# Where the activations lie in SBUF: 64 bytes later, and 272-token tiles 1,152 bytes apart

## The reference

```python
def first_block(...):                       # 272 tokens
    h = concatenate([meta, x])
    h += _mixer_rglru_swa(rmsnorm(h) ...)   # in0: projection, recurrence, windowed attention; out0
    h += swiglu(rmsnorm(h) ...)             # gu0: 1024 -> 2 x 2816, dn0: 2816 -> 1024
    h += _mixer_retention(rmsnorm(h) ...)   # in1: 1024 -> 6144, out1: 2048 -> 1024
    h += swiglu(rmsnorm(h) ...)             # gu1, dn1 (256 tokens from here on)
    return h[:, N_META:]

def second_block(x, ...):                   # 256 tokens, two layers
    x += 0.5 * rms_norm(swiglu(rms_norm(x), ffn1...))
    x += rms_norm(hybrid_mixer(rms_norm(x) ...))      # three attentions, gates, w_out
    x += 0.5 * rms_norm(swiglu(rms_norm(x), ffn2...))

def swiglu(x, wg, wu, wd):
    return (silu(x @ wg) * (x @ wu)) @ wd
```

## Time and profile before

| what | value |
|---|---|
| median of three runs | 2012.21 us |
| profiled execution, first to last instruction (span) | 2011.9 us |
| PE busy | 1998.7 us, 99% |
| PEld busy | 1755.0 us, 87% |
| DVE / ACT / POOL busy | 59% / 49% / 15% |
| mean granted TensorE clock | 0.997 |
| HBM read | 341.10 MB, 170 GB/s over the span |

### The profile page before, as it was taken

How to read it: one execution, slowest core, us unless ns; L and a number is a source line. 1 busy time by engine, 2 the same in 40 slices (tenths; PEclk the granted TensorE clock), 3 DMA queues, 4 the chain that set the end, 5 groups by cost and what they waited for, 6 DMA issues and landing times.

```text
span 2011.9 us, 27800 instructions
## 1 busy us (share of the span) xinstructions
PE 1998.7 (99%) x11810; PEld 1755.0 (87%) x11810; DVE 1178.9 (59%) x1133; ACT 990.8 (49%) x1076; POOL 303.7 (15%) x204
## 2 busy tenths in 40 slices
PE   9999999999999999999999999999999999999998
PEld 8899999999999988887888888888888888888887
DVE  6854446757654455546566865546555556686553
ACT  6753334345544354445356564446444535666443
POOL 4034401514344010002100110001000210011000
PEclk9999999999999999999999999999999999999999
DMA  7345556544555555554543445554556554354553
GB/s 223 105 138 176 167 179 201 168 129 144 186 177 181 188 187 184 185 197 159 176 147 126 167 168 188 188 209 159 185 180 209 168 167 146 112 209 154 183 180 136
DMA packets 195587, 343.67 MB, mean 171 GB/s; under 512 B 14122, under 2 KB 97356, under 8 KB 195356
## 3 DMA queue, kind: packets, MB, share of 16 engines
q1 hardware_dynamic: 194844, 340.12, 51.3%
q0 software_dynamic: 368, 0.79, 0.2%
q10 hardware_dynamic: 272, 1.26, 0.2%
HBM read 341.10 MB, written 1.05 MB: 170 GB/s over the span
## 4 chain that ended last, share of the span: by engine, by line
PE 91%; DVE 4%; ACT 3%; DMA 1%; POOL 1%; issue 0%; SPq 0%; DVEq 0%; POOLq 0%; ACTq 0%
PE banks L557 18%; PE banks L560 17%; PE banks L558 17%; PE banks L397 7%; PE banks L399 7%; PE banks L398 7%; PE banks L448 5%; PE banks L1778 2%; PE banks L1779 2%; PE banks L1780 2%; DVE w_lo L391 1%; PE banks L596 1%; PE banks L1869 1%; PE banks L1871 1%; PE banks L1870 1%; ACT w_hi L375 1%
## 5 line engine op out<-in xcount | busy, mean ns | idle before, releaser
L391 DVE TENSOR_TENSOR w_lo<-raw,w_hi 128x2048 fp32r<-128x2048 f32 x307 | 730.5, 2382 | 514.5 <-ACT w_hi L375 514.0
L375 ACT ACTIVATE w_hi<-raw 128x2048 fp32r<-128x2048 f32 x311 | 593.8, 1913 | 648.3 <-DMA raw<-ffn_wd 149.6
L557 PE MATMUL banks<-w_hi,xn_hi 128*128 128x512 f32 x1192 | 471.9, 396 | 0.9 <-DVE xn_lo L818 0.5
L558 PE MATMUL banks<-w_lo,xn_hi 128*128 128x512 f32 x1192 | 464.1, 389 | 0.0
L560 PE MATMUL banks<-w_hi,xn_lo 128*128 128x512 f32 x1192 | 459.6, 390 | 0.0
L557 PEld LDWEIGHTS banks<-w_hi,xn_hi 128*128 128x128 f32 x1192 | 223.9, 188 | 49.3 <-DVE w_lo L391 3.0
L560 PEld LDWEIGHTS banks<-w_hi,xn_lo 128*128 128x128 f32 x1192 | 223.8, 188 | 47.6
L558 PEld LDWEIGHTS banks<-w_lo,xn_hi 128*128 128x128 f32 x1192 | 224.1, 188 | 44.0
L397 PE MATMUL banks<-xn_hi,w_hi 128*128 128x272 f32 (+1 forms) x720 | 208.4, 289 | 0.5 <-DVE w_lo L1162 0.5
L399 PE MATMUL banks<-xn_hi,w_lo 128*128 128x272 f32 (+1 forms) x720 | 207.1, 288 | 0.0
L398 PE MATMUL banks<-xn_lo,w_hi 128*128 128x272 f32 (+1 forms) x720 | 206.7, 287 | 0.0
(11 more groups left out here) (371 smaller groups left out, 3079.1 us busy)
## 6 DMA issues: line engine op xcount, KB each, us to landing
raw<-w_in SPq DMA_DIRECT2D x58, 1024.0 KB, 5.1
raw<-ffn_wd SPq DMA_DIRECT2D x44, 1024.0 KB, 4.8
raw<-ffn_w_gu SPq DMA_DIRECT2D x42, 1024.0 KB, 4.9
raw<-ffn_wu SPq DMA_DIRECT2D x40, 1024.0 KB, 5.0
raw<-ffn_wg SPq DMA_DIRECT2D x35, 1024.0 KB, 5.0
raw<-ret_w_in SPq DMA_DIRECT2D x24, 1024.0 KB, 5.1
raw<-ffn_w_down SPq DMA_DIRECT2D x22, 1024.0 KB, 4.8
raw<-ret_w_out SPq DMA_DIRECT2D x8, 1024.0 KB, 5.4
```

Source lines behind the costliest of these rows:

```text
L375: nc.scalar.activation(hi_of(n0), raw_of(n0), ACT.Copy).then_inc(hi_done(n0), 1)
L391: nc.vector.tensor_tensor(lo_of(n0), raw_of(n0), hi_of(n0).bitcast(F32), ALU.subtract).then_inc(lo_done(n0), 1)
L557: pe.matmul(ps[:, (b + n) * 512:(b + n + 1) * 512], xh, h, start=start, stop=False)
L558: pe.matmul(ps[:, (b + n) * 512:(b + n + 1) * 512], xh, o, start=False, stop=False)
```

## The change

Three things are done to the byte offsets, and the order and number of instructions stay as they were on each engine.

1. 64 bytes are skipped ahead of `hT`, so `hT`, `xn_hi`, `xn_lo`, `act_hi` and `act_lo` start at 64 modulo 512 (`act_lo` is now placed by `act_hi` being rounded to the phase of `hT`), `Y` and the constants behind it at 320. The weights stay at 0, and the extra chunks (`raw_x`, `lo_x`, `hi_x`) that lie inside the activations' memory are rounded up to a multiple of 512 of their own. The split attention output (`mo_hi`, `mo_lo`) is at 64 in all three places. The first two chunks of gu0, staged raw in `act_hi`'s memory, land at 64.
2. Tiles of 272 tokens in `xn_*` and `act_*` are 288 words (1,152 bytes) apart: tile k starts at 64 + 128 k modulo 512, an odd multiple of 64 for every k. In part of the retention projection, which starts 16 tokens (64 bytes) into the tile, the start becomes 128 (k + 1), an even multiple for every k. `y1_split` keeps its packed tiles.
3. Copies over several tiles now step over the gap: ScalarE's copy of 128x544 becomes 128x2x272, GpSimd's and VectorE's subtraction likewise, and one copy and one subtraction of 128x1088 become 128x4x272.

```diff
+TS = 288
...
+A_PHASE = 64
...
-            if name in ("act_hi", "act_lo"):
-                at[0] += (raw_at - at[0]) % 512
+            if name == "act_hi":
+                at[0] += (hT_at - at[0]) % 512
...
-        hT, _ = new("hT", [P, KT, T1])
-        xn_hi, xn_at = new("xn_hi", [P, KT * T1], F32R)
-        xn_lo, _ = new("xn_lo", [P, KT * T1], F32R)
-        act_hi, a_at = new("act_hi", [P, NFF * T1], F32R)
-        act_lo, _ = new("act_lo", [P, NFF * T1], F32R)
+        at[0] += A_PHASE
+        hT, hT_at = new("hT", [P, KT, T1])
+        xn_hi, xn_at = new("xn_hi", [P, KT * TS], F32R)
+        xn_lo, _ = new("xn_lo", [P, KT * TS], F32R)
+        act_hi, a_at = new("act_hi", [P, NFF * TS], F32R)
+        act_lo, _ = new("act_lo", [P, NFF * TS], F32R)
...
-        raw_x, lo_x, hi_x = ([... for b, at0 in enumerate((extra_at, a_at))]
+        raw_x, lo_x, hi_x = ([... for b, at0 in enumerate((extra_at - extra_at % 512 + 512, a_at - a_at % 512 + 512))]
...
-        mo_hi, mo_lo = ([... (qn_at, vn2_at, e2_at)[x] ...
+        mo_hi, mo_lo = ([... (qn_at, vn2_at, e2_at + (a_at - e2_at) % 512)[x] ...
...
-                last = product(e, ..., xn_hi[:, kt * t:(kt + 1) * t], xn_lo[:, kt * t:(kt + 1) * t], ...)
+                last = product(e, ..., trow(xn_hi, kt, t), trow(xn_lo, kt, t), ...)
...
-                    c = (xt0 + 2 * k + j) * t
+                    c = (xt0 + 2 * k + j) * pitch(t)
...
+        def pitch(t):
+            return TS if t == T1 else t
+        def trow(x, kt, t, lo=0):
+            return x[:, kt * pitch(t) + lo:kt * pitch(t) + t]
+        def trows(x, kt, n, t):
+            return x[:, kt * pitch(t):(kt + n) * pitch(t)].rearrange("p (k s) -> p k s", s=pitch(t))[:, :, 0:t]
...
-                    at0 = (k0 - 1) * t
-                    dst = act_hi[:, at0:at0 + 2 * t] ...
-                    act.activation(dst, g, ACT.Copy).then_inc(S["ah"], 1)
+                    st = pitch(t)
+                    at0 = (k0 - 1) * st
+                    dst = act_hi[:, at0:at0 + 2 * st] ...
+                    act.activation(tiles(dst, st)[:, :, 0:t], tiles(g, t), ACT.Copy).then_inc(S["ah"], 1)
...
-                pool.tensor_tensor(lo, g, hi.bitcast(F32), ALU.subtract).then_inc(S["al"], 1)
+                pool.tensor_tensor(tiles(lo, st)[:, :, 0:t], g3, tiles(hi, st)[:, :, 0:t].bitcast(F32),
+                                   ALU.subtract).then_inc(S["al"], 1)
...
-                    xh, xl = xn_hi[:, kt * T1 + lo:(kt + 1) * T1], xn_lo[:, kt * T1 + lo:(kt + 1) * T1]
+                    xh, xl = trow(xn_hi, kt, T1, lo), trow(xn_lo, kt, T1, lo)
```

More of the change, by code:

```diff
@@ L229, in build_program @@
         extra_at = y_at + 4 * 7 * D
[L230 removed]
+        raw_x, lo_x, hi_x = ([place(f"{name}{b}", [P, CH], dt, at0 + off) for b, at0 in enumerate((extra_at - extra_at % 512 + 512, a_at - a_at % 512 + 512))]
                              for name, dt, off in (("raw_x", F32, 0), ("lo_x", F32R, 0), ("hi_x", F32R, 4 * CH)))
@@ L275, in build_program @@
         e2, p2, t1b, t2b = layer_map(e2_at, [("e2", [P, 4 * 384]), ("p2", [P, 4 * 384]), ("t1b", [P, 4, T2]), ("t2b", [P, 4, T2])], y_end)
-        mo_hi, mo_lo = ([place(f"mo_{part}{x}", [P, 4 * T2], F32R, (qn_at, vn2_at, e2_at)[x] + q * 16 * T2) for x in range(3)]
+        mo_hi, mo_lo = ([place(f"mo_{part}{x}", [P, 4 * T2], F32R, (qn_at, vn2_at, e2_at + (a_at - e2_at) % 512)[x] + q * 16 * T2) for x in range(3)]
                         for q, part in enumerate(("hi", "lo")))
@@ L496, in act_fill @@
                     act.wait_ge(S["pe_chunk"], base)
-                act.activation(xn_hi[:, kt * t:(kt + 1) * t], hv(kt, off, t), ACT.Copy,
+                act.activation(trow(xn_hi, kt, t), hv(kt, off, t), ACT.Copy,
                                scale=gcol[:, g0 + kt:g0 + kt + 1]).then_inc(S["xh"], 1)
@@ L504, in dve_fill @@
             dve.wait_ge(S["xh"], 8 * f + kt + 1)
-            c = slice(kt * t, (kt + 1) * t)
-            dve.scalar_tensor_tensor(out=xn_lo[:, c], in0=hv(kt, off, t), scalar=gcol[:, g0 + kt:g0 + kt + 1],
-                                     in1=xn_hi[:, c].bitcast(F32), op0=ALU.mult, op1=ALU.subtract).then_inc(S["xl"], 1)
+            dve.scalar_tensor_tensor(out=trow(xn_lo, kt, t), in0=hv(kt, off, t), scalar=gcol[:, g0 + kt:g0 + kt + 1],
+                                     in1=trow(xn_hi, kt, t).bitcast(F32), op0=ALU.mult, op1=ALU.subtract).then_inc(S["xl"], 1)
         def dve_residual(w, fill=None, off=0, t=T1, between={}):
@@ L1078, in fill_hi @@
                 act.wait_ge(S["xT"], kt + 1)
-                act.activation(xn_hi[:, kt * T1:(kt + 1) * T1], ps[:, kt * 512:kt * 512 + T1], ACT.Copy,
+                act.activation(trow(xn_hi, kt, T1), ps[:, kt * 512:kt * 512 + T1], ACT.Copy,
                                scale=gcol[:, G_MIX0 + kt:G_MIX0 + kt + 1]).then_inc(S["xh"], 1)
@@ L1165, in first_fill @@
                 dve.wait_ge(S["xh"], kt + 1)
-                c = slice(kt * T1, (kt + 1) * T1)
-                dve.scalar_tensor_tensor(out=xn_lo[:, c], in0=ps[:, kt * 512:kt * 512 + T1], scalar=gcol[:, G_MIX0 + kt:G_MIX0 + kt + 1],
-                                         in1=xn_hi[:, c].bitcast(F32), op0=ALU.mult, op1=ALU.subtract).then_inc(S["xl"], 1)
+                dve.scalar_tensor_tensor(out=trow(xn_lo, kt, T1), in0=ps[:, kt * 512:kt * 512 + T1],
+                                         scalar=gcol[:, G_MIX0 + kt:G_MIX0 + kt + 1], in1=trow(xn_hi, kt, T1).bitcast(F32), op0=ALU.mult, op1=ALU.subtract).then_inc(S["xl"], 1)
             dve.wait_ge(S["vecT"], 1)
@@ L1658, in heads_hi @@
                 act.wait_ge(S["pv0"], g + 1)
-                at0, b = (4 + 2 * g) * T1, GROUP_BANKS[g][0]
-                act.activation(tiles(xn_hi[:, at0:at0 + 2 * T1], T1), bank(b, 2)[:, :, 0:T1], ACT.Copy).then_inc(S["xcat_h"], 1)
+                b = GROUP_BANKS[g][0]
+                act.activation(trows(xn_hi, 4 + 2 * g, 2, T1), bank(b, 2)[:, :, 0:T1], ACT.Copy).then_inc(S["xcat_h"], 1)
             split_hi(base + 2, 0)
@@ L1708, in act_l0 @@
             act.wait_ge(S["scan"], 1)
-            act.activation(tiles(xn_hi[:, 0:4 * T1], T1), lt[:, :, :], ACT.Copy).then_inc(S["yrnh"], 1)
+            act.activation(trows(xn_hi, 0, 4, T1), lt[:, :, :], ACT.Copy).then_inc(S["yrnh"], 1)
             split_hi(out0 + 2, 0)
```

32 lines of the change are left out of this document (16 added, 16 removed).

## The result

The changed kernel is slower. It takes 2034.28 us, the median of 4 runs (2033.01 to 2036.71), against 2011.99 us for the kernel before (4 runs, 2011.77 to 2013.87). The ratio is 1.011, with a 95% interval of 1.0097 to 1.0122, so 22.3 us more where the forecast was 17.3 less. The two profiled executions lie closer together, since that of before was its slowest and that of after its fastest: 2013.87 against 2033.01 us, spans of 2011.9 and 2031.2. (A span is 1.8 to 2.0 us shorter than the time of the same execution.

A forecast was written before the change was run, and what follows sets the result against it. TensorE was taken as the bound: number of matmuls times start-to-start distance. Terms -11.2, -3.5, -3.5, -0.3 and +1.2 us sum to -17.3, from 2012.2 to 1994.9 us; the 8-in-10 range was 1966 to 2017.

The forecast's parts named there:

- weakest term: 512-column matmuls: stationary activations moving from 0 to 64 save 2.2 ns on each of 5088, -11.2 us.
- an overhead of 13.3 ns at either width: Per-matmul cost beyond one cycle per column, read from 256 columns in gu1, dn1 and 512 in the second block.
- Bound: Whole kernel: TensorE is busy 1998.7 of 2011.9 us at full clock, idle 1.2 us at most before any group.
- gu1 and dn1: 256-column matmuls: moving activations going from 0 to 64 save 2.2 ns on each of 1584, -3.5 us.
- 272 columns of `xn`: All tiles at odd multiples of 64 instead of half: 1.6 ns less on each of 2160 matmuls, -3.5 us.
- `act`: 272-column matmuls of the gated activations, all tiles odd instead of half: 0.6 ns less on 528, -0.3 us.
- The 11.1 ns: Assumed overhead of a tile at an odd multiple of 64, a weighted mean from gu0, dn0, in1 and out1.
- in1 at 256 columns: All tiles at even multiples of 64 instead of half: 2.0 ns more on 576 matmuls, +1.2 us.
- out1: 256-column matmuls, half odd and half even starts before and after: no change on 384.
- Edits at nothing: Copies and subtractions over the gap stay under idle time; the subtraction TensorE waits for may cost tenths of a microsecond.
- the slower one: Rival, 512-column matmuls: the shifted stationary operand collides more, 16.6 ns overhead, +16.8 us there, 2023 us; chance 0.15.
- The forecast's own range: Whole kernel: 1985 to 2005 us around the forecast, for odd-start overheads of 9.5 to 12.5 ns.

The follow-up runs named there:

- e1: Changed kernel with the second block's normalised input and gated activations back at 0 modulo 512; 2008.61 us, 0.9981 of the kernel before.
- e5: Changed kernel with the weights also moved 64 bytes and the second block's normalised input at 0; 2015.85 us.
- e13: As e12, with 272-token tiles of the normalised input 1,280 bytes apart, each starting 64 bytes before a multiple of 256; 2002.74 us, 0.9946 of the kernel before.
- e15: As e13, but the first block's activations start at a multiple of 256 bytes, as the weights do; 2010.47 us.
- e6: Changed kernel with each 512-column matmul of the second block cut into two of 256, and its gated activations at 0; 2033.84 us.
- e8: Changed kernel with the second block's normalised input at 16 bytes and its gated activations at 384; 2032.54 us.
- e12: The same kernel as e9, timed in 7 runs; 2007.43 us, 0.9962 of the kernel before.
- e9: Changed kernel with first-block activations 192 bytes after the weights' start, second block's normalised input and gated activations at that start; 2000.48 us in one run.

## Why the prediction was wrong

**The step that failed** is the one the text called its weakest term: "that an odd start of the stationary operand acts like one of the moving operand is taken over from the other case". It gave the 5088 matmuls of 512 columns -11.2 us. Measured, they went from 227.3 to 233.3 ns, 5.97 x 5087 = +30.4 us. Against that, steps that were long anyway shrank from 16.0 to 10.7 us above the median. Of these 5.3 us some 3.0 are the wait and the low clock at 908 us of before; that slower matmuls cover more of the other waits is a guess for the rest. Together +25.0 us. The experiments say what the step mixed up. Not the start of an operand counts but D, and D has a sign (229.0 against 233.3 ns at 512 columns), which changes when the roles swap. And the price depends on the width: 256 columns are cheaper at every other D than 0 (or as dear, at -96), 512 columns are cheapest at 0. The prediction had read "an overhead of 13.3 ns at either width" and concluded that overhead and width are apart. That is true at D = 0 alone. At +64 the part above 0.417 ns a column is 6.6 or 11.1 ns at 256 columns and 20 ns at 512.

The Trainium skill ("TensorE: Matmul & The Clock Gate", Step-by-step: what each phase is for) was weighed on this: by it a weight load comes through a read port of its own and takes no bandwidth from the running matmul. The prediction drew from it that the addresses are of no account, and that e1 and e5 contradict, with 6 ns for 64 bytes of one operand and none when both move. So the prediction was right to set the rule aside, for what turned out to be the wrong sign.

Point by point:

- **Bound**: right. The same count, and 10.9 us not busy. The clock was not quite at its full level "in every slice", since a 9 in a slice stands for 90% or more (the 3.4 us at 908), and the longest idle time before a group is 2.0 us (`ysb`), not 1.2.
- **gu1 and dn1**, forecast -3.5 us: 120.0 to 117.8 ns, -3.5. Right in size. The reason given, that odd starts are cheaper, holds only as D = -64.
- **272 columns of `xn`**, forecast -3.5 us at 124.5 ns: 126.06 to 125.20, 0.86 x 2160 = -1.9. `act`: forecast -0.3, measured 0.0 (125.2 both times). The 11.1 ns were twice a mixture less 13.3, that is, one price for odd tiles and one for even; e13 to e15 show that at this width the relation at a constant start gives other numbers than at 256.
- **in1 at 256 columns**, forecast +1.2 us at 120.0 ns, called the sharpest test: 117.86 to 118.69, 0.83 x 576 = +0.5. The sign is right, the size is under half. All its tiles start at even multiples of 64 now, but with a pitch of 1,152 every second one has D = 128, which costs 118.7 in the table and not 120.0. "Even" lumped 0 and 128 together. Half and half makes 119.3; the measured 118.7 is below that too, so the mixture of starts is not simply their mean.
- **out1**, forecast 0: 117.78 to 118.61, +0.3 us. Its packed tiles go through the same four values of D before and after, beginning at another one, so the mean over D does not account for this either.
- **Sum**: -3.5 - 1.9 + 0.5 + 0.3 = -4.6 for the first block, where the timeline has -4.5. With +25.0 for the 512 columns and -1.2 for all other steps of the second block that is the +19.3 of the span. Of the -1.2, 0.8 are the eight small matmuls at the lower clock in before.
- **Edits at nothing**: right. ScalarE's copy over the gap takes 634 to 660 ns, 646 before, and stays under idle time:

```profile
L994 ACT ACTIVATE act_hi<-ffn_g 128x544 f32 x10 | 6.6, 660 | 37.7 <-DVE ffn_g L973 37.7
L994 ACT ACTIVATE act_hi<-ffn_g 128x512 f32 x10 | 6.3, 634 | 33.5 <-DVE ffn_g L973 33.5
```

- **The rivals**: the slower one had the place, the direction and the operand right ("the load starts 64 bytes ahead of the moving stream in place of behind it"), with a chance of 0.15. Its price, 16.6 ns, came from the longest single step of gu0; measured were 20 ns, so its 2023 was short of 2034. The forecast's own range was also summed too narrow: overheads of 9.5 to 12.5 ns, on 9360 matmuls, make 1980 to 2008 us and not 1985 to 2005. The whole range stopped at 2017 although the price at 512 columns was unknown and the text had worked out 2046. With 5088 matmuls on a term that no row shows, and an end of 2046, the range should have reached it, and the sign should have been near even.

What stays open: why the same pair of addresses has two levels at 256 columns, and what picks one; why 272 columns differ from 256; what beside D moves stages whose tiles change their start (in1, out1); whether the first output column counts, which in in1 lies 16 columns into its bank and in gu1 at its start; and which part of the memory or of the load path is behind it all. The two levels inside e6 change at a boundary between groups of matmuls, which suggests that the history before a stretch decides, but no run varied that alone.

## What to carry to other kernels

Where a kernel is bound by matmuls that follow each other without a gap, and each brings its own stationary tile, lay stationary and moving tiles out as a pair: with equal starts modulo 256 bytes for 512 columns, and for 256 columns at unequal starts. The stationary tile 64 bytes after the moving one was best there, 113.3 ns in some executions and 117.8 in others; no start gave 113.3 every time. A stage in which the two operands swap roles needs its own layout; shifting "all activations" improved one stage here and damaged the other. A gain measured on one operand at one width is no evidence for the other operand or another width, and an unshown price on half of all matmuls belongs in the range at both its ends.

## What the runs showed of the hardware

- Sixteen bytes between the starts of a stationary and a moving tile cost 5.6 ns, 2.5%, of every 512-column matmul (227.4 ns in before, 233.0 in e8). The step does not grow with the distance: 233.2 at 32, 233.3 at 64, 232.4 to 233.1 at 128. On the other side, at -64, it is 229.0 to 229.1.
- Several of the steady distances are whole multiples of 16 cycles of 2.4 GHz: 113.3 ns is 272 cycles, 120.0 is 288, 126.7 is 304, 233.3 is 560. At 512 columns and D = 0, where steps of 227 and 226 ns follow each other two to one, the undisturbed distance is 226.7 ns, 544 cycles. Sixteen cycles are sixteen columns, which are 64 bytes of float32. Others are not (117.8 ns is 282.7), and that the 64 bytes are the cause is only a guess.
- One program has two times: 2000 to 2002 and 2007 to 2010 us in e12, in seven runs on one chip at a granted clock of 0.996 to 0.998, and e13 likewise (1998.38 to 2000.1 and 2005.38 to 2006.76). The traces of this program (e9, e12) show it as 113.3 or 117.8 ns in gu1; of e13 only an execution of the longer group was traced, with 117.8. A single run of such a kernel can be 7 us off.
- No stage in any run came below 113.3 ns for 256 columns, 6.7 ns above one cycle a column.
- Behind one idle stretch of 1.98 us, TensorE's granted clock was at 1.2 GHz for 3.4 us: eight matmuls of 128 columns took 1.62 us there and 0.79 at the full clock of the other trace.
